# Decode-step kernel: x joined in the last group of the expert sums, their first group made expert by expert, group norms side by side, samples modulated in wide operations

## The reference

```python
def layer(x, c, ...):
    sh1, sc1, g1, sh2, sc2, g2 = jnp.split(jax.nn.silu(c) @ w_ada + b_ada, 6, axis=-1)   # one row per sequence
    h = rms_norm(x, norm1_w) * (1 + sc1) + sh1
    mix = token_mixer(h, ...)
    x = x + g1 * mix
    h = rms_norm(x, norm2_w) * (1 + sc2) + sh2
    return x + g2 * peer(h, ...)

# end of token_mixer
y = rms_norm(y.reshape(b, L, 2, 512), ssm_norm_w)        # two groups of 512 channels
merged = jax.nn.sigmoid(ga) * (o_attn @ w_br_attn) + jax.nn.sigmoid(gs) * (y @ w_br_ssm)
return merged @ w_out

# peer: 16384 experts of one neuron, 16 chosen per token and head
act = gelu(einsum('thkd,td->thk', peer_u[e], xb))
out = einsum('thk,thkd->td', g * act, peer_v[e])

y_prompt, y_sample = rms_norm(x, norm_f_w)
```

## Time and profile before

| | us |
|---|---|
| median of 3 runs | 4880.0 |
| the profiled execution | 4877.53 |
| its span, first to last instruction | 4875.6 |
| TensorE busy | 4503.4 (92%) |
| VectorE busy | 2893.8 (59%) |
| ScalarE busy | 1339.6 (27%) |
| GpSimd busy | 910.0 (19%) |
| mean granted TensorE clock | 0.95 of full |

### The profile page before, as it was taken

How to read it: one execution, slowest core, us unless ns; L and a number is a source line. 1 busy time by engine, 2 the same in 40 slices (tenths; PEclk the granted TensorE clock), 3 DMA queues, 4 the chain that set the end, 5 groups by cost and what they waited for, 6 DMA issues and landing times. The chain is left out here.

```text
span 4875.6 us, 71419 instructions
## 1 busy us (share of the span) xinstructions
PE 4503.4 (92%) x26288; PEld 2714.0 (56%) x26288; DVE 2893.8 (59%) x5214; ACT 1339.6 (27%) x1823; POOL 910.0 (19%) x982
## 2 busy tenths in 40 slices
PE   5999979998767997999999999999996999999995
PEld 2666634443444564666666666666663555555553
DVE  5465313444554445326666666666545898888984
ACT  3232213333111001223444444443222222122221
POOL 0000013321000010000000000000004666666640
PEclk8999989998776998999999999999998999999998
DMA  4533423322323455224645555555447888888861
GB/s 178 188 132 141 158 70 94 86 77 67 104 87 145 149 186 188 74 99 152 210 168 199 188 193 185 180 207 180 154 137 263 306 296 290 302 292 296 298 219 74
DMA packets 397656, 854.93 MB, mean 175 GB/s; under 512 B 42514, under 2 KB 233618, under 8 KB 388562
## 3 DMA queue, kind: packets, MB, share of 16 engines
q1 hardware_dynamic: 274162, 470.37, 28.9%
q0 software_dynamic: 78752, 283.31, 17.1%
q10 hardware_dynamic: 44480, 97.93, 5.4%
HBM read 673.44 MB, written 178.03 MB: 175 GB/s over the span
## 5 line engine op out<-in xcount | busy, mean ns | idle before, releaser
L373 PE MATMUL dot_ps<-h_parts,u_parts 128*128 128x384 f16 (+1 forms) x9216 | 1454.0, 317 | 7.5 <-PEq L1979 4.9
L373 PEld LDWEIGHTS dot_ps<-h_parts,u_parts 128*128 128x128 f16 x9216 | 893.0, 98 | 499.3 <-issue 8.2
L373 PE MATMUL totals_ps<-act_parts,v_parts 128*128 128x416 f16 x6144 | 1084.3, 340 | 37.2 <-DVE act_parts L2900 33.3
L373 PEld LDWEIGHTS totals_ps<-act_parts,v_parts 128*128 128x128 f16 x6144 | 602.0, 98 | 518.2 <-issue 37.0
L386 PE MATMUL in_ps<-h_parts_in,in_parts 128*128 128x384 f16 (+1 forms) x3168 | 492.6, 318 | 4.9 <-DVE in_parts L713 4.5
L2615 DVE SCALAR_TENSOR_TENSOR u_parts<-u_chunks,units,u_parts 128x1024 f16<-128x1024 f32 x126 | 161.8, 1284 | 515.9 <-ACT u_parts L2399 515.9
L2408 ACT ACTIVATE gelu<-dot_ps,units 128x384 f32<-128x384 f32 (+1 forms) x384 | 216.3, 564 | 803.2 <-PE dot_ps L373 803.1
L386 PEld LDWEIGHTS in_ps<-h_parts_in,in_parts 128*128 128x128 f16 x3168 | 309.5, 98 | 182.3 <-DVE in_parts L713 4.6
L2967 POOL DMA_INDIRECT row_value<-tmp_g_rows,row_g x256 | 304.6, 1190 | 394.0 <-POOLq L2273 316.2
L2856 ACT ACTIVATE v_parts<-v_group,units 128x1024 f16<-128x1024 f32 x128 | 136.6, 1139 | 773.5 <-PE totals_ps L373 740.7
L2911 DVE SCALAR_TENSOR_TENSOR h<-totals_ps,sum_unit,h 128x416 f32<-128x416 f32 x388 | 248.0, 648 | 142.0 <-PE totals_ps L373 138.4
(11 more groups left out here) (365 smaller groups left out, 5395.7 us busy)
## 6 DMA issues: line engine op xcount, KB each, us to landing
u_chunks<-in_u SPq DMA_DIRECT2D x128, 512.0 KB, 5.5
v_sweep<-in_v SPq DMA_DIRECT2D x128, 512.0 KB, 4.6
v_group<-in_v SPq DMA_DIRECT2D x32, 2048.0 KB
tmp_g<-gelu ACTq DMA_DIRECT2D x128, 416.0 KB, 2.7
tmp_w<-h POOLq DMA_DIRECT2D x26, 2048.0 KB, 8.2
w_groups<-tmp_w SPq DMA_DIRECT2D x32, 1664.0 KB
gelu_in<-tmp_g SPq DMA_DIRECT2D x32, 1664.0 KB
merge_sweep<-in_u POOLq DMA_DIRECT2D x64, 512.0 KB, 7.7
```

The lines of the kernel that those rows point to most:

```text
L373: mm = pe.matmul(bank, left(x), right(y), start=first and x == 0 and y == 0, stop=last and x == 1)
```

## The change

There are four parts.

1. **Norm and merge.** `Norm` can have its own `rstd` and banks, and its ScalarE part is split in `squares` and `roots`. Group 1 gets a tile `rstd_group` and banks 3 to 5. ScalarE squares both groups, then takes both roots; TensorE adds up both, one behind the other. `banks_taken` is set free after the mean, root and reciprocal of group 0. In a round TensorE makes the attention products of all three splits first and the products with y after them; in the loop's first half it waits for all 8 chunks of y only between the two.
2. **modulated.** The two operations on the samples are done once, over all 8 chunks (512 elements per partition), behind the last L269.
3. **First group of the sums.** The loads of v and gl of group 0 come expert by expert (8 transfers in place of 2, each pair with a semaphore of its own), and ScalarE and VectorE work on an expert when its pair is there.
4. **x joined in the last group.** SyncE loads x behind the last `load_g`, into buffers that have become free (v's slot 0, w's slot 0, the row buffers). VectorE adds x to `acc` times the gate within the last group: chunks 0 to 2 after m = 5, 3 to 5 after m = 6, 6 and 7 after m = 7. The final phase has no load and no addition left, and norms `acc` in place.

```diff
-    def __init__(self, nc, sem, name, src, squares, s, psum, chunks=KC):
+    def __init__(self, nc, sem, name, src, squares, s, psum, chunks=KC, rstd=None):
...
+    def squares(self, act, loaded=None):
         for k in range(self.chunks):
...
+    def scalar(self, act, loaded=None):
+        self.squares(act, loaded)
+        self.roots(act)
...
     for k in range(KC):
         dve.tensor_tensor(dst[:, k, :], src[:, k, :], s["rstd"][:, :], ALU.mult).then_inc(scaled, 1)
-        dve.wait_ge(scaled, k + 1)
-        own = dst[:, k, SEQ:T].rearrange("p (s l) -> p s l", l=LS)
-        link(dve.tensor_tensor(own, own, per_seq(gain, k), ALU.mult))
-        dve.tensor_tensor(own, own, per_seq(sh, k), ALU.add)
+    dve.wait_ge(scaled, KC)
+    own = dst[:, :, SEQ:T].rearrange("p k (s l) -> p k s l", l=LS)
+    link(dve.tensor_tensor(own, own, per_seq(gain), ALU.mult))
+    dve.tensor_tensor(own, own, per_seq(sh), ALU.add)
...
             def _(pe):
                 group[0].tensor(pe)
-                pe.wait_ge(y_ready, 1)
                 group[1].tensor(pe)
-                pe.wait_ge(y_ready, 2)
                 pe.wait_ge(o_in, 16)
...
+                        if u == 0:
+                            pe.wait_ge(y_ready, KC)
+                        for j, (t0, n) in enumerate(SPLITS):
...
-                group[0].scalar(act)
-
-                act.wait_ge(y_ready, 1)
-                group[1].scalar(act)
+                group[0].squares(act)
+                group[1].squares(act)
+                group[0].roots(act)
+                group[1].roots(act)
...
+        GATED_AT = {5: (0, 1, 2), 6: (3, 4, 5), 7: (6, 7)}
+        x_slots = [v[:, 0, :, :].rearrange("p j d -> p (j d)"), w[:, 0, :, :, :].rearrange("p b e t -> p (b e t)"),
+                   spare[:, :, :].rearrange("p r d -> p (r d)")]
...
-                load_g(0)
-                load_v(0, 0)
+                for j in range(GRP):
+                    sp.dma_start(v[:, 0, j, :], a["v"][0, :, j, :]).then_inc(first_in[j], 16)
+                    sp.dma_start(gl[:, j, :], a["g"][j]).then_inc(first_in[j], 16)
                 load_w(1, 1)
                 load_v(1, 1)
+
+                def load_x():
+                    for k in range(KC):
+                        if k == 0:
+                            sp.wait_ge(v_split, LAST * GRP)
+                        if k == 3:
+                            sp.wait_ge(a_split, LAST * GRP)
+                        if k == 6:
+                            sp.wait_ge(row_added, 1 + NROWS)
+                        sp.dma_start(x_of(k), a["x_mid"][:, k, :]).then_inc(x_in, 16)
...
                     load_g(g + 1)
+                    if isinstance(g, int) and g == LAST - 1:
+                        load_x()
...
+                def first_parts():
+                    for j in range(GRP):
+                        act.wait_ge(first_in[j], 32)
+                        lead_v(0, j)
+                        if j > 0:
+                            lead_a(0, 0, j - 1)
+                    lead_a(0, 0, GRP - 1)
...
+                def gated(k):
+
+                    if k == 0:
+                        dve.wait_ge(back_taken, BACKS)
+                        dve.wait_ge(x_in, 16 * KC)
+                    dve.wait_ge(held_taken, k // 2 + 1)
+                    dve.wait_ge(sum_taken, BANKS + LAST * MOVED + (k + 1) * ND - (k + 1) // 2)
+                    x, to, gate = x_of(k), acc[:, k, :], s["mod"][:, 5 * KC + k, :]
+                    dve.scalar_tensor_tensor(to[:, 0:SEQ], to[:, 0:SEQ], gate[:, 0:1], x[:, 0:SEQ], ALU.mult, ALU.add)
...
-                weigh(0, 0, 0, range(GRP))
-                rest_v(0, 0, range(GRP))
-                rest_a(0, 0, range(GRP))
+                for j in range(GRP):
+                    weigh(0, 0, 0, (j,))
+                    rest_v(0, 0, (j,))
+                    if j > 0:
+                        rest_a(0, 0, (j - 1,))
+                rest_a(0, 0, (GRP - 1,))
...
-        x = ctx.enter_context(nc.sbuf_tensor("x_end", [P, KC, T], F32))
+        x = s["acc"]
```

More of the change, by code:

```diff
@@ L246, in vector @@
             dve.wait_ge(self.summed, i + 1)
-            dve.tensor_scalar(self.s["rstd"][:, t0:t0 + n], self.psum[:, i, 0:n], 1.0 / (self.chunks * P), EPS,
+            dve.tensor_scalar(self.rstd[:, t0:t0 + n], self.psum[:, i, 0:n], 1.0 / (self.chunks * P), EPS,
                               ALU.mult, ALU.add).then_inc(self.meaned, 1)
@@ L1821, in merge_phase @@
         HALF_C = KC // NG
+        rstds = [s["rstd"], sb("rstd_group", [P, T])]
         group = [Norm(nc, sem, f"group{g}", y[:, g * HALF_C:(g + 1) * HALF_C, :],
-                      h[:, g * HALF_C:(g + 1) * HALF_C, :], s, ps, HALF_C) for g in range(NG)]
+                      h[:, g * HALF_C:(g + 1) * HALF_C, :], s, ps[:, g * NS:(g + 1) * NS, :], HALF_C, rstds[g])
+                 for g in range(NG)]
         norm = Norm(nc, sem, "norm2", x, y, s, ps)
@@ L1912, in _ @@
                     group[g].vector(dve)
+                    if g == 0:
+                        dve.sem_inc(banks_taken, NS)
                     for c in range(g * HALF_C, (g + 1) * HALF_C):
@@ L2750, in sums_phase, with x_of @@
         LOOPS = (NGRP - 2) // 2
+        x_in = sem("x_in2")
+        first_in = [sem(f"first_group_in{j}") for j in range(GRP)]
+        GATED_AT = {5: (0, 1, 2), 6: (3, 4, 5), 7: (6, 7)}
+        x_slots = [v[:, 0, :, :].rearrange("p j d -> p (j d)"), w[:, 0, :, :, :].rearrange("p b e t -> p (b e t)"),
+                   spare[:, :, :].rearrange("p r d -> p (r d)")]
+        def x_of(k):
+            return x_slots[k // 3][:, k % 3 * T:(k % 3 + 1) * T]
         def flat(x):
@@ L2849, in _, with lead_v, lead_a @@
             def _(act):
+                def lead_v(r, j):
+                    act.activation(v16[:, r, 0, j, :], v[:, r, j, :], ACT.Copy,
+                                   scale=units[:, V_SCALE:V_SCALE + 1]).then_inc(v_hi, 1)
+                def lead_a(g, r, j):
+                    act.wait_ge(weighed, g * GRP + j + 1)
+                    act.activation(flat(a16[:, r, 0, j, :]), w[:, r, :, j, :], ACT.Copy,
+                                   scale=units[:, A_SCALE:A_SCALE + 1]).then_inc(a_hi, 1)
+                def first_parts():
[5 more added lines that the diff above has]
+                    lead_a(0, 0, GRP - 1)
                 def parts(g, r, i):
-                    if not isinstance(g, int) or g > 0:
-                        act.wait_ge(sum_done, g * PER)
-                    act.wait_ge(v_in[r], i * 16 + 16)
+                    act.wait_ge(sum_done, g * PER)
+                    act.wait_ge(v_in[r], i * 16 + 16 * r)
                     for j in range(GRP):
-                        act.activation(v16[:, r, 0, j, :], v[:, r, j, :], ACT.Copy,
-                                       scale=units[:, V_SCALE:V_SCALE + 1]).then_inc(v_hi, 1)
+                        lead_v(r, j)
                     for j in range(GRP):
-                        act.wait_ge(weighed, g * GRP + j + 1)
-                        act.activation(flat(a16[:, r, 0, j, :]), w[:, r, :, j, :], ACT.Copy,
-                                       scale=units[:, A_SCALE:A_SCALE + 1]).then_inc(a_hi, 1)
+                        lead_a(g, r, j)
                 def turn(g, r, i):
@@ L2886, in weigh @@
                             dve.wait_ge(w_in[r], i * 16 + 16)
-                            dve.wait_ge(g_in, g * 16 + 16)
+                        if isinstance(g, int) and g == 0:
+                            dve.wait_ge(first_in[j], 32)
+                        elif j == 0:
+                            dve.wait_ge(g_in, g * 16)
                         x = w[:, r, :, j, :]
@@ L2947, in turn @@
                         add(g, m)
+                        if g == LAST:
+                            for k in GATED_AT.get(m, ()):
+                                gated(k)
+                def gated(k):
[6 more added lines that the diff above has]
+                    dve.scalar_tensor_tensor(to[:, 0:SEQ], to[:, 0:SEQ], gate[:, 0:1], x[:, 0:SEQ], ALU.mult, ALU.add)
+                    own = to[:, SEQ:T].rearrange("p (q l) -> p q l", l=LS)
+                    link.link(dve.tensor_tensor(own, own, gate[:, 1:].unsqueeze(2).to_broadcast([P, NSEQ, LS]),
+                                                ALU.mult))
+                    dve.tensor_tensor(to[:, SEQ:T], to[:, SEQ:T], x[:, SEQ:T], ALU.add)
                 dve.sem_inc(sum_taken, BANKS)
@@ L2988, in final_phase @@
     with ExitStack() as ctx:
-        x = ctx.enter_context(nc.sbuf_tensor("x_end", [P, KC, T], F32))
+        x = s["acc"]
         squares = ctx.enter_context(nc.sbuf_tensor("squares_end", [P, KC, T], F32))
-        spare = ctx.enter_context(nc.sbuf_tensor("spare_end", [P, 2, NSEQ, LS], F32))
         ps = ctx.enter_context(nc.psum_tensor("end_ps", [P, NS, 512], F32))
-        x_in, x_ready, y_ready, y_out, chain = (
-            sem("x_in2"), sem("x_ready"), sem("y_final"), sem("y_out"), sem("final_chain"))
```

(8 more changed lines are left out.)

19 lines of the change are left out of this document (9 added, 10 removed).

## The result

The changed kernel takes 4840.1 us (median of 4 runs, 4834.3 to 4842.6) against 4880.7 before: ratio 0.9917, 95% interval 0.9904 to 0.9929. It is 40.6 us faster; the forecast was 43.7 us and 4836.3. In a later measurement the same kernel stood at 4835.9 against 4879.2, 43.3 us less.

A forecast was written before the change was run, and what follows sets the result against it. TensorE, busy 92% of the span, was taken as the bound, with gains only where chains keep it waiting. 19.3 + 17.4 + 7.0 + 0 = 43.7 us off the 4880.0 median gave 4836.3 us, range 4827 to 4849.

The forecast's parts named there:

- The end: Final phase: x joined within the last group of the sums lets the squares begin 19.3 us sooner.
- no wait for x: End: joins wait only for ScalarE's last copy; rival, a late x, 5%, up to 13.3 us back, 4849.6.
- the same low clock at the norm: End: after 9 us idle the norm's products restart at the lower clock, again 16.73 us; 2 us possible, not taken.
- Merge: Start of merge: group 1's mean 10.1 us sooner, attention products covered for 7.3 us; 17.4 us together.
- the rival of rounds that stall on VectorE: Merge: TensorE waits for VectorE in 7 later rounds, paying 71 us, 4907; chance 3%.
- modulated: Ends of ada and merge: block takes 11.1 us instead of 14.6, 3.5 us won twice, 7.0 us.
- the bound of doubled wide operations: modulated: if four-dimensional access doubled the wide operations, 1.4 us less won each time.
- The first group: Start of the sums: TensorE starts 3.9 us earlier but resumes at the same 3735.14; gain taken as 0.
- the pace of 390 GB/s: First group of the sums: rate at which v landed, used to place the arrivals of the four load pairs.
- TensorE waits 7.8 us in place of 3.84: First group of the sums: longer wait for additions behind group 1's gelu values; resumption unchanged, 0 us.
- The rule on small transfers: First group of the sums: 2.0 us fixed per DMA; six extra, serialized, add 12 us; rival, 4848, 7%.
- The step that I left out: Second norm, first product to first mean: not worked out in the prediction, change put at 0 us.

The follow-up runs named there:

- part 1 alone: Kernel before the change with only the group norms side by side and merge's attention products ahead: 4862.6 us, ratio 0.9967.

## Why the prediction was right, and where it was off

- **The end** (19.3 us) measured 19.7, 19.5 as a kernel of its own. Joins of 1.6 us, no wait for x, TensorE not held, the same low clock at the norm: each step as worked out. The squares begin 19.4 us sooner against the last product; the other 0.3 us is in the norm's products, 16.9 us long in this trace and 17.3 before.
- **Merge** (10.1 + 7.3 us) measured 10.3 + 7.9 in this pair of traces. The rounds cost nothing more, 276.29 against 276.32 us; the rival of rounds that stall on VectorE fell.
- **modulated** (2 x 3.5 us) measured 3.45 and 3.44. Operations on 512 elements took 0.69 us, so the bound of doubled wide operations fell too.
- **The first group** (0 us) is right in its mechanism: the start moved, the resumption didn't. Two steps of it were off. The pairs came later than at the pace of 390 GB/s (the last at 23.2 us after the first load, not 19.3), so TensorE gained 1.8 us, not 3.9, and waited 6.2 us, not 7.8. And "TensorE waits 7.8 us in place of 3.84" was costed at nothing, though the clock fell in all five traces with the longer gap and only in two of five with the shorter one. It cost 1.9 us on average, of which the clock explains a part.
- **The rule on small transfers** (the Trainium skill, DMA: Bandwidth & Descriptors, section Anatomy of one DMA), taken one transfer behind another, would have added 12 us. TensorE started earlier, not later, and the values of group 1 landed 0.8 us later in this pair of traces. The trace decides against that reading for this queue; the Trainium skill doesn't say there that queued transfers follow one another, and its figure was measured on transfers issued from GpSimd, where these come from SyncE. That the pairs were 3.9 us later than at the old pace may be a part of it; holding 2 MB of rows back moved the last pair by only 0.3 us, so what delays the pairs stays open.
- **The step that I left out** is the second norm. I asked for the clock at gaps that the change makes or leaves, not at one that it doesn't touch. The term was put at nothing without a look at it. It cost 2.7 us in the profiled execution and 1.7 us in others.

In this pair of traces the stretches that have to do with the change add up to 3.45 + 18.11 + 0.03 - 2.74 + 3.44 - 1.73 + 19.73 = 40.3 us, against 40.6 between the medians. The 3.4 us missing from 43.7 are the 4.5 lost at the second norm and in the first group of the sums, less the 1.1 that merge and the end won beyond their forecasts. That 40.3 and 40.6 agree so closely is in part luck: in the same two traces the stretches with nothing of the change in them add up to 5.4 us the other way, and the spans differ by 34.9 us.

## What to carry to other kernels

When an engine is released earlier, look for the next thing that it needs before you count the gain: here the same transfer ended the wait in both kernels, and only once the next group's values stood ahead of 2 MB that nobody needed yet did the earlier start pay, 1.65 us of it. A gap of a few microseconds of TensorE can have a price of its own at restart, some 1.5 to 3.2 us here, and one that you don't change may still begin to cost. A few products on constants in such gaps, into a bank that is free, gave 5 us in three places. Size such a gain on the kernel that you build on: its price here was not the same in every trace.

## What the runs showed of the hardware

The granted clock at the same 3.49 us gap, with the same instructions on every engine for some 120 us ahead of it (the 8 rounds with w_out), fell in all seven traces that had the attention products ahead and no filler, and in none of the five without them. In the changed kernel's first trace and with part 1 alone the fall came 1.1 to 1.3 us before TensorE's restart (16.5 us to the first mean), in the five others 0.6 to 0.8 us behind it (15.44 us). What carries the difference over these 120 us was not settled. In the first group of the sums gaps of 2.54 to 3.03 us kept the clock in three traces, but one of 2.02 us lost it, as did 3.84 us and all five of 4.6 to 6.4 us: the length of the last gap alone does not decide. In the first group the fall came from 2.7 us before the restart to 0.5 us behind it.
